# Two mixers' queries and keys turned by VectorE and a DRAM buffer instead of TensorE, and a streamed chunk's products in the order of their kinds

## What is computed

```python
# first layer
proj = rmsnorm(h) @ w_in                       # 2048 x 20528
h_a  = mlstm(q_a, k_a, v_a, i, f); h_a = norm(h_a) * sigmoid(o) * silu(z)
h_b  = gated_delta(conv_silu(qkv), beta, g)
h    = h + sigmoid(gate_a) * (h_a @ w_out[:2048]) + sigmoid(gate_b) * (h_b @ w_out[2048:])
# two layers like this
h    = x @ w_in2
y    = concat(band(a_q, a_k, a_v) * silu(a_z), gla(b_q, b_k, b_v) * silu(b_z), memory_attention(m_q, mem @ w_mem_kv) * silu(m_z))
x    = layer_norm(ALPHA * x + y @ w_out2)
```

## Time and profile before

| | us |
|---|---|
| median of 3 runs | 2139.01 |
| profiled execution, its own time | 2139.0 |
| its span | 2137.4 |
| TensorE (PE) busy | 2118.9 (99%) |
| VectorE (DVE) busy | 1312.0 (61%) |
| ScalarE (ACT) busy | 1108.1 (52%) |
| GpSimd (POOL) busy | 156.2 (7%) |

### The profile page before, as it was taken

How to read it: one execution, slowest core, us unless ns; L and a number is a source line. 1 busy time by engine, 2 the same in 40 slices (tenths; PEclk the granted TensorE clock), 3 DMA queues, 4 the chain that set the end, 5 groups by cost and what they waited for, 6 DMA issues and landing times.

```text
span 2137.4 us, 29849 instructions
## 1 busy us (share of the span) xinstructions
PE 2118.9 (99%) x10852; PEld 1753.3 (82%) x10852; DVE 1312.0 (61%) x1745; ACT 1108.1 (52%) x1468; POOL 156.2 (7%) x256
## 2 busy tenths in 40 slices
PE   9999999999999999999999999999999999999998
PEld 7888888888888787888878888888888788888886
DVE  6456556464553877787776565566546845567467
ACT  6554545454444848474755454445444544545453
POOL 7000000000000100000010000100001211000012
PEclk9999999999999999999999999999999999999999
DMA  9866566666565555454556765755658567555654
GB/s 337 269 182 214 172 213 195 199 198 217 179 206 184 148 157 169 143 173 139 177 144 220 254 185 170 226 146 170 193 181 302 181 204 193 167 162 182 200 178 159
DMA packets 211584, 411.00 MB, mean 192 GB/s; under 512 B 14096, under 2 KB 31009, under 8 KB 211070
## 3 DMA queue, kind: packets, MB, share of 16 engines
q1 hardware_dynamic: 199440, 369.94, 55.7%
q0 software_dynamic: 9712, 30.98, 4.6%
q10 hardware_dynamic: 2304, 8.39, 1.1%
HBM read 395.19 MB, written 14.07 MB: 191 GB/s over the span
## 4 chain that ended last, share of the span: by engine, by line
PE 85%; DVE 6%; ACT 4%; issue 4%; DMA 1%; DVEq 0%; ACTq 0%; SPq 0%
PE stream_psum L663 26%; PE stream_psum L665 25%; PE stream_psum L664 25%; ACT work L1101 2%; PE heads_psum L633 2%; DVE w_low L1531 2%; ACT w_high L1101 2%; DVE work L1717 1%; PE heads_psum L1018 1%; PE heads_psum L981 1%; PE heads_psum L962 1%; DMA w_raw<-in_w_mem_kv 1%; PE heads_psum L784 0%; ACT L1101 0%; DVE work L1783 0%
## 5 line engine op out<-in xcount | busy, mean ns | idle before, releaser
L1531 DVE TENSOR_TENSOR w_low<-w_raw,w_high 128x1024 fp32r<-128x1024 f32 x688 | 829.7, 1224 | 641.0 <-ACT w_high L1101 639.0
L1101 ACT ACTIVATE w_high<-w_raw 128x1024 fp32r<-128x1024 f32 x688 | 711.1, 1057 | 465.9 <-PE stream_psum L665 387.1
L663 PE MATMUL stream_psum<-w_high,x_high 128*128 128x512 f32 x1856 | 739.7, 399 | 0.2
L665 PE MATMUL stream_psum<-w_high,x_low 128*128 128x512 f32 x1856 | 724.6, 390 | 0.0
L664 PE MATMUL stream_psum<-w_low,x_high 128*128 128x512 f32 x1856 | 723.8, 390 | 0.0
L663 PEld LDWEIGHTS stream_psum<-w_high,x_high 128*128 128x128 f32 x1856 | 349.1, 188 | 74.2 <-issue 2.2
L665 PEld LDWEIGHTS stream_psum<-w_high,x_low 128*128 128x128 f32 x1856 | 348.7, 188 | 73.3
L664 PEld LDWEIGHTS stream_psum<-w_low,x_high 128*128 128x128 f32 x1856 | 349.2, 188 | 69.8 <-issue 1.9
L663 PE MATMUL stream_psum<-w_high,y_high 128*128 128x512 f32 x896 | 354.0, 395 | 3.1 <-DVE y_low L1990 3.1
L665 PE MATMUL stream_psum<-w_high,y_low 128*128 128x512 f32 x896 | 350.3, 391 | 0.0
L664 PE MATMUL stream_psum<-w_low,y_high 128*128 128x512 f32 x896 | 350.2, 391 | 0.0
(11 more groups left out here) (321 smaller groups left out, 1269.1 us busy)
## 6 DMA issues: line engine op xcount, KB each, us to landing
w_raw<-in_w_in SPq DMA_DIRECT2D x528, 512.0 KB, 4.4
w_raw<-in_w_out SPq DMA_DIRECT2D x128, 512.0 KB, 4.9
w_raw<-in_w_mem_kv SPq DMA_DIRECT2D x32, 512.0 KB, 5.4
turned_scratch<-work POOLq DMA_DIRECT2D x40, 128.0 KB, 3.4
work<-turned_scratch POOLq DMA_DIRECT2D x10, 512.0 KB, 5.6
work<-rows_scratch POOLq DMA_DIRECT2D x8, 512.0 KB, 5.9
proj<-in_mem_t SPq DMA_DIRECT2D x8, 256.0 KB, 7.0
work<-in_x_t SPq DMA_DIRECT2D x4, 512.0 KB, 6.7
```

What stands on the lines that cost most here:

```text
L663: pe.matmul(acc, hi[:, k, sl(m)], w, start=first, stop=False)
L665: return pe.matmul(acc, lo[:, k, sl(m)], w, start=False, stop=final)
L1101: return act.activation(dst, src, func, **kw)
L1531: tt(WL[:, c % RING, :], RAW[:, c % RING, :], WH[:, c % RING, :].bitcast(F32), ALU.subtract).then_inc(lo_done, 1)
```

## The change

Four parts. First, `ml` and the kinds `m` and `a` of `attend` (for `a` its first use in a layer; the second becomes kind `b` and stays as it was) turn queries and keys with VectorE's 32x32 transposes and a trip by DRAM (`keys_across`); ScalarE and VectorE then copy them from `work` into place. In numbers: 4 x 8 + 2 x 16 + 2 x 16 = 96 transposes of TensorE go. In `ml` the scores move from step 6 to step 13 and the values from step 10 to step 17; in `attend` the scores move from step 5 to step 23. Second, in `dn` the transposes of the values and of the keys' first half (`v`, `k0t`) come one step later, and the steps behind them stand where they stood. Third, the 12 matmuls of a chunk go by kind: 4 high x `w_high`, then 4 low x `w_high`, then 4 high x `w_low`; the chunk's start waits for `w_high` alone, and the last four wait for `w_low`. Fourth, `turned_scratch` has two buffers.

```diff
+            def keys_across(n, at, to):
+                both = len(at)
+                for i in range(both):
+                    store_turned(i, at[i], keys_out)
+                wait_alone(pool, keys_out, n * 64 + 64 * both)
+                for i in range(both):
+                    pool.dma_start(wk(to[i]), turned_d[i]).then_inc(keys_in, 16)
...
             with pool.Fori(1, 4) as g:
+                wait_alone(pool, *done(ML_V, "turned_qk", g - 1))
+                keys_across(g - 1, (4,), (5,))
...
+                pool.wait_ge(*done(AT_V["m"], "turned_qk", l))
+                keys_across(4 + 4 * l, (2, 3), (4, 5))
...
# TensorE, stream
-                        pe.wait_ge(lo_done, n + (b * per + c + 1))
-                        for kk in range(CH):
-                            for m in range(M):
-                                last = passes(c, kk, m)
-                            if kk == CH - 1:
-                                last.then_inc(used, 1)
-                            advance(side)
+                        pe.wait_ge(hi_done, n + (i + 1))
+                        for kk, m in places:
+                            pe.matmul(acc(m), hi[:, tiles[c] + kk, sl(m)], WH[:, i % RING, sl(kk, NBLK)], start=(c, kk) == (0, 0), stop=False)
+                        for kk, m in places:
+                            if (kk, m) == (1, 0):
+                                advance(side)
+                            pe.matmul(acc(m), lo[:, tiles[c] + kk, sl(m)], WH[:, i % RING, sl(kk, NBLK)], start=False, stop=False)
+                        pe.wait_ge(lo_done, n + (i + 1))
+                        for kk, m in places:
+                            last = pe.matmul(acc(m), hi[:, tiles[c] + kk, sl(m)], WL[:, i % RING, sl(kk, NBLK)], start=False, stop=(c, kk) == (per - 1, CH - 1))
+                        last.then_inc(used, 1)
+                        advance(side)
...
# TensorE, ml
-                for i, n in enumerate("qk"):
-                    for h in range(2):
-                        for m in range(M):
-                            last = tr(H[:, i, h * S + m * P:h * S + (m + 1) * P], PR[:, m, i * S + h * P:i * S + (h + 1) * P])
-                    last.then_inc(*signal(ML_PE, n))
-                yield from gap(3)
+                yield from gap(10)
...
# TensorE, dn
-                yield from gap(6)
+                yield from gap(7)
                 pe.wait_ge(*done(DN_V, "conv133", g))
                 project(2, 0).then_inc(*signal(DN_PE, "v"))
-                yield from gap(9)
+                yield from gap(8)
...
-                yield from gap(6)
+                yield from gap(7)
                 pe.wait_ge(*done(DN_V, "nk", g))
...
# ScalarE, ml
-                act.wait_ge(*done(ML_PE, "q", g))
-                f(wk(0, 512), bank(0), ACT.Copy, scale=float(P) ** -0.5).then_inc(*signal(ML_ACT, "q"))
-                act.wait_ge(*done(ML_PE, "k", g))
-                f(wk(0.5, 512), bank(1), ACT.Copy).then_inc(*signal(ML_ACT, "k"))
+                yield from gap(11)
+                wait_alone(act, keys_in, g * 16 + 16)
+                for i, n in enumerate("qk"):
+                    for h in range(2):
+                        last = f(wk(i / 2 + h / 4, S).rearrange("p (m a t) -> p m a t", m=M, a=4), by_features(5)[:, 2 * i + h], ACT.Copy, scale=1.0 if i else float(P) ** -0.5)
+                    last.then_inc(*signal(ML_ACT, n))
...
# VectorE, ml
+                dve.wait_ge(evac, 8 * g + (2 * (E_ML + 1)))
+                turn(PR[:, :, 0:NBLK], 4).then_inc(*signal(ML_V, "turned_qk"))
+                yield
...
-                yield from gap(3)
+                yield from gap(13)
                 dve.wait_ge(*done(ML_ACT, "expw", g))
...
# VectorE, attend, kinds m and a
+                    turn(PR[:, :, 0:NBLK], 2)
+                    turn(wk(9, 2 * U).rearrange("p (m n) -> p m n", m=M)[:, :, 0:NBLK] if full else PR[:, :, NBLK:2 * NBLK], 3).then_inc(*signal(AT_V[kind], "turned_qk"))
...
+                    yield from gap(17)
+                    l, i = divmod(q - 8, 4)
+                    dve.wait_ge(keys_in, 16 * (4 + 4 * l + 2 * max(0, i - 1) + 2))
```

More of the change, by code:

```diff
@@ L92, in build @@
     rel_d = nc.dram_tensor("rel_scratch", (A_H, COPIES, BIASW), F32, kind="Internal").ap()
-    turned_d = nc.dram_tensor("turned_scratch", (P, U), F32, kind="Internal").ap()
+    turned_d = [nc.dram_tensor(f"turned_scratch{i}", (P, U), F32, kind="Internal").ap() for i in range(2)]
     memt_d = [nc.dram_tensor(f"mem_{n}_scratch", (P, KT, S), F32, kind="Internal").ap() for n in ("high", "low")]
@@ L525, in _ @@
                 across(g - 1, 9, 10)
+            pool.wait_ge(*done(ML_V, "turned_qk", 3))
+            keys_across(3, (4,), (5,))
             pool.wait_ge(*done(ML_V, "turned", 3))
@@ L590, in _ @@
                                    bass.AP(rel_d.tensor, P - 1 - p, [[BIASW - 1, COPIES], [COPIES * BIASW, A_H], [1, S]])).then_inc(rel_bw, 16)
-                for i in range(2):
-                    pool.wait_ge(*done(AT_V["a"], "turned", 2 * l + i))
+                pool.wait_ge(*done(AT_V["a"], "turned_qk", l))
+                keys_across(6 + 4 * l, (2, 3), (4, 5))
+                for i, kind in enumerate("ab"):
+                    pool.wait_ge(*done(AT_V[kind], "turned", l))
                     across(5 + 3 * l + i, 8, 7)
@@ L826, in dn @@
                 last.then_inc(*signal(DN_PE, "k0t"))
-                yield from gap(2)
+                yield
                 def quarters(at, left, right):
@@ L1330, in attend @@
                 f(wk(8).rearrange("p (m n) -> p m n", m=M), PR[:, :, sl(zslot, NBLK)], ACT.Tanh, scale=0.5).then_inc(*signal(act_s, "tz"))
-                act.wait_ge(*done(steps, "q", n))
-                f(wk(0), bank(2, 2), ACT.Copy, scale=float(P) ** -0.5).then_inc(*signal(act_s, "q"))
+                l, i = divmod(q - 8, 4)
+                if kind == "b":
+                    act.wait_ge(*done(steps, "q", n))
+                    f(wk(0), bank(2, 2), ACT.Copy, scale=float(P) ** -0.5).then_inc(*signal(act_s, "q"))
+                else:
+                    yield from gap(18)
+                    act.wait_ge(keys_in, 16 * (4 + 4 * l + 2 * max(0, i - 1) + 2))
+                    for h in range(4):
+                        last = f(wk(h / 4, S).rearrange("p (m a t) -> p m a t", m=M, a=4), by_features(4)[:, h], ACT.Copy, scale=float(P) ** -0.5)
+                    last.then_inc(*signal(act_s, "q"))
                 yield from gap(4)
@@ L1867, in attend @@
                 after_side(dve, q)
-                dve.wait_ge(*done(steps, "k", n))
-                dve.tensor_copy(wk(1), bank(0, 2)).then_inc(*signal(AT_V[kind], "k"))
+                if kind == "b":
+                    dve.wait_ge(*done(steps, "k", n))
+                    dve.tensor_copy(wk(1), bank(0, 2)).then_inc(*signal(AT_V[kind], "k"))
+                else:
+                    dve.wait_ge(evac, evac_need)
+                    if full:
+                        dve.wait_ge(kv_in, (q - 8) * 16 + 64)
+                    turn(PR[:, :, 0:NBLK], 2)
+                    turn(wk(9, 2 * U).rearrange("p (m n) -> p m n", m=M)[:, :, 0:NBLK] if full else PR[:, :, NBLK:2 * NBLK], 3).then_inc(*signal(AT_V[kind], "turned_qk"))
+                    yield
                 G = wk(8).rearrange("p (m n) -> p m n", m=M)
@@ L1872, in attend @@
                 stt(G, G, 1.0, PR[:, :, sl(zslot, NBLK)], ALU.add, ALU.mult).then_inc(*signal(AT_V[kind], "g"))
+                if kind != "b":
+                    yield from gap(17)
+                    l, i = divmod(q - 8, 4)
+                    dve.wait_ge(keys_in, 16 * (4 + 4 * l + 2 * max(0, i - 1) + 2))
+                    for h in range(4):
+                        last = dve.tensor_copy(wk(1 + h / 4, S).rearrange("p (m a t) -> p m a t", m=M, a=4), by_features(5)[:, h])
+                    last.then_inc(*signal(AT_V[kind], "k"))
                 yield from gap(3)
@@ L1903, in attend @@
                 dve.wait_ge(*done(AT_V[kind], "fg", n))
-                turn(7, 8).then_inc(*signal(AT_V[kind], "turned"))
+                turn(wk(7).rearrange("p (m n) -> p m n", m=M), 8).then_inc(*signal(AT_V[kind], "turned"))
                 yield from gap(13)
```

80 lines of the change are left out of this document (45 added, 35 removed).

## The result

The changed kernel takes 2171.7 us (median of 4 runs, 2169.1 to 2174.4), the kernel before beside it 2139.3 (4 runs): ratio 1.0154, 95% interval 1.0142 to 1.0167. It is 32 us slower; 2175 was forecast, in a range of 2149 to 2189. The profiled execution took 2169.1 us (span 2167.4), 30 more than that of before.

The account below looks back on a forecast made before the run. TensorE, busy for 99% of the span, was taken to bound the kernel. The terms -10.6 + 16.0 + 16.0 + 16.0 - 0.8 - 0.7 = +35.9 on 2139.0 us gave 2174.9 us, range 2149 to 2189.

Parts of the forecast that it names:

- Transposes, -10.6: Transposes leaving TensorE save 0.9 us in each first-mixer group and 1.76 in each of four attention sides: -10.6 us.
- Scores, +16.0: First mixer: TensorE waits for the DRAM trip before the scores, 4.0 us (between 1.5 and 5.1) in four groups: +16.0.
- An estimate by the rule of the Trainium skill: First mixer's trip: 3.2 us each half, copies end at 164.3, scores don't wait, total about 2151; the prediction rejected it.
- Values, +16.0: First mixer: a block's end delays exponent, mask and product, so TensorE waits 4.0 us before the values, four times: +16.0.
- Clock, +16.0: TensorE's clock falls to 1.2 GHz behind the eight new waits, 2.0 us lost for each: +16.0 (0 to 22.4).
- Attention, 0: Memory and band attention: copies end near 26 us, scores needed 31.3 us behind the boundary, no wait: 0 (to +25.6).
- Delta turns, -0.8: In `dn` idle times of 0.47 and 0.35 us vanish, at most 0.28 kept, the rest waited for at L864: -0.8.
- Order of kinds, -0.7: Chunk's matmuls: first products start earlier, at half clock, -0.7 us (0 to -1.4); eight matmuls hide the mixer's late `w_low`.

Follow-up runs that it names:

- The filled waits: The changed kernel with matmuls whose results nobody reads (16, or 8) ahead of each of TensorE's eight waits in the first mixer: 2161.7 us, ratio 1.0107.
- the run with attention sooner: The kernel before with attention's trips alone (2133.1 us), and in it the copies and scores of the four attention sides 2 chunks sooner: 2134.3 us.
- chunks 8 and 10: The changed kernel with the first mixer's scores and values 2 chunks later, in chunks 8 and 10 of the stream: 2132.1 us, ratio 0.9965.
- chunks 10 and 12: The changed kernel with the first mixer's scores and values each 4 chunks later, in chunks 10 and 12 of the stream: 2137.8 us, ratio 0.999.
- the product a chunk earlier: The kernel with chunks 8 and 10, and in it exponent, mask and product one chunk earlier in ScalarE's and VectorE's queues: 2130.1 us, ratio 0.9955.

## Why the prediction was right, step by step

- **Transposes, -10.6.** Right: 0.90 us for each of four mixer groups, 1.78 for each of four attention sides.
- **Scores, +16.0.** Measured 13.25. The trip was read rightly: 12.9 us where the mixer's own trip gave 13.6, and copies of 1.33 for 1.71. The 4.0 was a choice between 5.1 and 1.5, and the reason given for it, emptier queues, is not shown by any run. Three groups waited 3.6 to 3.9; the fourth has another order on ScalarE, which I had not looked at. An estimate by the rule of the Trainium skill (page "DMA: Bandwidth & Descriptors", section "Anatomy of one DMA"), 3.2 us for each half of the trip, does not hold here: the halves took 5.6 and 6.6 us, beside a stream that moves 185 to 200 GB/s.
- **Values, +16.0.** Measured 15.50: the queue behind the block's end, link by link.
- **Clock, +16.0.** Measured by subtraction: the four groups have 59.5 us over 2.72 a chunk, of which 16.0 is left where nothing waits (91.03 a group), and 28.75 are the waits; 14.8 are left, and 26.6 us at 1.2 GHz are worth half of that, 13.3. The filled waits showed the cause and the same size, about 13. The rest, 1 to 2 us, the prediction had put at nothing: a wait costs some 0.3 us beyond its idle time, as the waits of 0.88 us show at full clock. The clock fell behind the seven waits of 3.6 to 3.9 us, twice as long behind one of them as behind the others, so the 2.0 us each are a mean. The Trainium skill (page "TensorE: Matmul & The Clock Gate", section "HAM oscillation") told it in kind. The trace agrees: the granted clock is 0.50 behind seven of the eight waits.
- **Attention, 0.** Right, and the estimate of 26 us for the trip too (26.2 to 27.0 by the run with attention sooner).
- **Delta turns, -0.8.** The term is off by size: of the 0.2 us a group that it keeps, nothing was kept. The mechanism is the one named: the stall passed to L864 when these turns were changed alone.
- **Order of kinds, -0.7.** The size was off both ways: -2.9 in the profiled execution, because the shorter idle time kept the clock up, and 0 over the runs. Its other half, that eight matmuls hide the late `w_low` in the mixer, was right. In the kernel forecast that is worth next to nothing, since the wait of 0.88 us only takes the place of a part of the wait for the scores; where the scores don't wait it is worth 3.6 us.

For the profiled execution the terms add up to 6 us less than forecast (+29.9 for +35.9), nearly all of them in one direction: 2.8 at the scores, 2.2 at the start, 1.2 at the clock, 0.5 at the values, against 0.8 at the delta turns. That execution is the fastest of its four; the median comes within 3.2 us of the forecast, and this last bit of closeness is luck, not a better sum.

The sum of the parts alone (+42.1 mixer, -6.1 attention, +0.4 delta, +0.5 kinds = +36.9) is 4 above the whole (+32.4). By the lengths of the groups 1.2 of it lies in the mixer (408.9 for 407.7), in groups one and four, whose scores' waits and clock differ; the rest is not resolved by these runs, and no more than the start moves between executions.

## What to carry to other kernels

Moving work off the bounding engine pays only if its consumer moves too: find the latest time at which the long way delivers and put the consumer behind it, and then check what has moved in front of the block's end. Eight waits of 1.9 to 3.9 us of the bounding engine cost themselves and, mostly through the clock, half as much again (28.75 and 14.8 us); waits of 0.5 to 1.3 us left it up (chunks 8 and 10). Matmuls for nobody in the long ones gave most of that part back. A wait ahead of another wait can be free: it is paid only when the later one is gone. And a stall of less than 1 us that is removed ahead of a chain that doesn't depend on it comes back at the chain's end.

## What was not expected

**ScalarE stops at the start.** In nine of fourteen profiled executions ScalarE stands still for 1.1 to 3.3 us somewhere between 48 and 55 us, ahead of a `w_high`, with nothing in the profile that it waits for. Timeline of ScalarE in the kernel with scores and values in chunks 10 and 12:

```profile
51.79 0.19 ACT L1129 ACTIVATION_READ_ACCUMULATOR work<-residual 128x1 f32 x1
55.23 1.06 ACT L1129 ACTIVATE w_high<-w_raw 128x1024 fp32r<-128x1024 f32 x1 [3.26 <-issue]
...
59.32 1.04 ACT L1129 ACTIVATE w_high<-w_raw 128x1024 fp32r<-128x1024 f32 x1
```

The block's copies to `proj` come later by as much (60.27 to 61.34), and TensorE stands still for 4.56 us until 61.43 and loses clock behind it. The profiled executions of the changed kernel and of the order of kinds alone have no such stop and are the fastest of their four and eleven; that of the kernel with chunks 8 and 10 has one of 3.28 us and is the slowest of its seven. The others fit less well: with 3.26 us, chunks 10 and 12 are the seventh of eleven, and with 1.75 the product a chunk earlier is the second fastest of five. So that the stop makes the spread over the runs is a guess. It occurs with and without each part of the change. The DMA engines are fully busy there (in the kernel before, a share of 1.05 between 45 and 57 us). In the stop above both of the profile's instruction queues carry a packet, at 52.66 and 55.12. The Trainium skill (page "Runtime: NRT & Kernel Launch", section "Instruction fetch mechanics") has an engine's next instructions come in blocks by DMA while it runs on. That speaks for a late block, but the traces don't bear it out: the changed kernel has the same two packets (50.89 and 53.26) and no stop, and the kernel with the delta turns alone stops for 1.94 us up to 50.58 with no such packet between 40 and 54.40. The cause stays open.

**Loads of weights come later beside the trips.** Where TensorE never waits in the mixer, ScalarE does, for `w_raw`. In the first group it does so five times, for 0.6 to 3.4 us, with the product a chunk earlier, and twice, for 3.05 and 0.95 us, in the kernel before. With chunks 10 and 12 it waits up to 5.34 us at once (above). It reached TensorE only at the places named.
